# Differential attention and retention in one Trainium2 kernel: the order in which TensorE takes up scores, transposes, sums and outputs

## The chip, the cores and the metric

The kernel runs on one core of one Trainium2 chip. The metric is the device time of one launch in microseconds (us); lower is better. Engine names as in the profile: PE is TensorE (PEld its weight loads), DVE is VectorE, ACT is ScalarE, POOL is GpSimd, SP is SyncE.

## What is computed

Two transformer blocks over 512 tokens of width 1024, in float32. The first mixes a retention branch and a differential attention branch, then runs a mixture of experts; the second has a sliding-window attention and a product-key expert layer. The change touches the two branches of the first block alone:

```python
def retention(q, k, v):                      # 4 heads, dk 128, dv 256, chunks of 128
    s = jnp.einsum('bnihd,bnjhd->bnhij', qc, kc) * dmask      # scores times a decay
    ...
    return (o_in + o_cross).reshape(B, S, H, dv)
ro = head_rms(ro)                            # o * rsqrt(mean(o * o) + EPS), per head

def diff_attention(q, k, v, lam):            # 4 heads, two score maps each
    ...
    p = jax.nn.softmax(s, axis=-1)
    a = p[:, :, 0] - lam * p[:, :, 1]
    return jnp.einsum('bhqk,bkhe->bqhe', a.astype(v.dtype), v)
do = head_rms(do) * diff_norm * (1.0 - lambda_init)
```

## The kernel before

The program is written by hand, engine by engine: each stage is a block with one instruction stream for each engine, and semaphores between them. An engine works through its stream in order, so an instruction that waits holds back all that stand behind it. A stage begins for all engines together when the one before is over.

**`stage_retention`** computes all of retention in its quadratic form, head by head (h = 0 to 3). PE makes four score tiles of the head (`scores(h)`, L585: 128 keys by 512, 384, 256 and 128 queries, two instructions for each in the trace). DVE multiplies them by the decay (`weigh(h)`, L639). PE multiplies by the values into two banks (L597: "output" below). ACT squares both banks (L546) into the buffer `squares`, of which there is one; PE sums the squares over the partitions with a matrix of ones (L604: "total"); ACT takes the root (L550) into `std`, of which there is one; DVE takes the reciprocal (L647) and multiplies both banks by it (L649): "norm" below. The stream of DVE is `weigh(0)`, `weigh(1)`, norm 0, `weigh(2)`, norm 1, `weigh(3)`, norm 2, some sums for lambda, norm 3. The stream of ACT is squares 0, root 0, squares 1, root 1, and so on; squares h wait for total h-1, and root h for norm h-1. `scores(h)` begins with

```python
if h >= 1:
    pe.wait_ge(s.weighted, TT * h)
```

that is, it waits until all of `weigh(h-1)` is done, and the output of head h waits for all of `weigh(h)`.

**`stage_diff`** computes differential attention in 16 units u = (h, t): head h, block t of 128 queries, which sees (t + 1) * 128 keys. For a unit, PE makes the scores of both maps (`scores(u)`, L809), DVE adds the mask and takes the largest (`softmax_max(u)`, L913 to L920, called max), ACT takes exponents with their sums (`exponents(u)`, L874), DVE combines the maps (L928 to L932, called mix), PE transposes the result block by block (`turn(u)`, L819), and ACT copies it out of the one transpose bank (L885). After a head's last unit PE makes the head's output (`output(h)`, L828), ACT squares it (`squares_of`, L860), PE sums (`total`, L837), ACT takes the root (`root_of`, L866), and DVE norms (`normed`, L900 and L902). Two units have score banks and buffers at a time: `scores(u+2)` waits for the exponents of u, and the exponents of u+2 for mix u. DVE's stream is max u+1, mix u, max u+2, mix u+1, and so on; ACT's is exponents u+1, copy u, exponents u+2, copy u+1. In both, the parts of the norm stand at fixed places behind some unit t of the next head. Exponents and roots need different tables of ACT, which shows as ACT_TABLE_LOAD.

Of the kernel before, what the change touches and what calls it, by code (L numbers as in the profile page):

```python
# [26 lines left out]
HEADS = 4  # L27
# [525 lines left out]
def stage_retention(nc, m, qT, kT, vals, roT):  # L553

    with ExitStack() as own:
        sb = lambda name, shape: own.enter_context(nc.sbuf_tensor(name, shape, F32))
        decay = sb("decay", [P, HEADS, T])
        probs = sb("ret_probs", [P, 2, TT, T])
        squares = sb("ret_sq", [P, 2, T])
        std = sb("ret_std", [P, T])  # L560
        lam_in, lam_p = sb("lam_in", [P, 4, P]), sb("lam_p", [P, P])
        lam_s, lam_e = sb("lam_s", [P, 2]), sb("lam_e", [P, 2])
        lam_loaded, lam_ready, lam_exp = (m.sem(f"lam_{x}") for x in ("loaded", "ready", "exp"))
        s = Names()
        s.decay, s.scores, s.weighted, s.out_ready, s.squares, s.total, s.root, s.normed = (
            m.sem(f"ret_{x}") for x in ("decay", "scores", "weighted", "out", "squares", "total", "root", "normed"))
        block = own.enter_context(nc.Block(no_gpsimd_drain=True))

        score = [m.bank[0][:, 0:T], m.bank[1][:, 0:T - P], m.bank[4][:, 0:T - 2 * P], m.bank[1][:, T - P:T]]
        o_banks = [[m.bank[6], m.bank[7]], [m.bank[3], m.bank[5]]]  # L570
        ss_bank = m.bank[2]

        @block.sync
        def _(sp):
            sp.dma_start(decay[:, :, :], m.dram.decay).then_inc(s.decay, 16)
            for i, a in enumerate(m.dram.lams):
                sp.dma_start(lam_in[:, i, :], a.to_broadcast([P, P])).then_inc(lam_loaded, 16)

        @block.tensor
        def _(pe):  # L580
            def scores(h):
                if h >= 1:
                    pe.wait_ge(s.weighted, TT * h)
                for j in range(TT):
                    pe.matmul(score[j], kT[:, h, j * P:(j + 1) * P], qT[:, h, j * P:T],  # L585
                              start=True, stop=True).then_inc(s.scores, 1)

            scores(0)
            for h in range(HEADS):
                if h + 1 < HEADS:  # L590
                    scores(h + 1)
                pe.wait_ge(s.weighted, TT * (h + 1))
                if h >= 2:
                    pe.wait_ge(s.normed, h - 1)
                for c in range(2):
                    for j in range(TT):
                        mm = pe.matmul(o_banks[h % 2][c][:, j * P:T], vals[:, j, h * DV + c * P:h * DV + (c + 1) * P],  # L597
                                       probs[:, h % 2, j, j * P:T], start=(j == 0), stop=(j == TT - 1))
                mm.then_inc(s.out_ready, 1)
                pe.wait_ge(s.squares, 2 * (h + 1))  # L600
                if h >= 1:
                    pe.wait_ge(s.root, h)
                for c in range(2):
                    mm = pe.matmul(ss_bank[:, :], m.ones, squares[:, c, :], start=(c == 0), stop=(c == 1))  # L604
                mm.then_inc(s.total, 1)

        @block.scalar
        def _(act):
            for h in range(HEADS):
                head_norm_act(m, act, o_banks[h % 2], ss_bank, squares, std, h, s)  # L610
            act.wait_ge(lam_ready, 1)
            act.activation(lam_e[:, :], lam_s[:, :], ACT.Exp).then_inc(lam_exp, 1)

        @block.vector
        def _(dve):
            chain = lambda instruction: m.chain(dve, instruction)

            def lambda_sums():
                dve.wait_ge(lam_loaded, 64)
                for i in range(2):  # L620
                    chain(dve.tensor_tensor(lam_p[:, :], lam_in[:, 2 * i, :], lam_in[:, 2 * i + 1, :], ALU.mult))
                    chain(dve.tensor_reduce(lam_s[:, i:i + 1], lam_p[:, :], AX.X, ALU.add))
                dve.sem_inc(lam_ready, 1)
                dve.tensor_scalar(m.dn[:, :], m.dn[:, :], 1.0 - LAMBDA_INIT, None, ALU.mult)

            def lambda_difference():
                dve.wait_ge(lam_exp, 1)
                chain(dve.tensor_tensor(m.neg_lam[:, :], lam_e[:, 1:2], lam_e[:, 0:1], ALU.subtract))
                chain(dve.tensor_scalar(m.neg_lam[:, :], m.neg_lam[:, :], LAMBDA_INIT, None, ALU.subtract))

            dve.wait_ge(s.decay, 16)

            def weigh(h):
                if h >= 2:
                    dve.wait_ge(s.out_ready, h - 1)
                for j in range(TT):

                    dve.wait_ge(s.scores, TT * h + (1 if j == 0 else TT))
                    dve.tensor_tensor(probs[:, h % 2, j, j * P:T], score[j],  # L639
                                      decay[:, h, 0:T - j * P], ALU.mult).then_inc(s.weighted, 1)  # L640

            weigh(0)
            for h in range(HEADS):
                if h + 1 < HEADS:
                    weigh(h + 1)
                dve.wait_ge(s.root, h + 1)
                chain(dve.reciprocal(std[:, :], std[:, :]))  # L647
                for c in range(2):
                    last = dve.tensor_tensor(roT[:, 2 * h + c, :], o_banks[h % 2][c][:, :], std[:, :], ALU.mult)  # L649
                last.then_inc(s.normed, 1)  # L650
                if h == HEADS - 2:
                    lambda_sums()
            lambda_difference()
# [129 lines left out]
def stage_diff(nc, m, qT, kT, vals, doT):  # L783

    units = [(h, t) for h in range(HEADS) for t in range(TT)]
    with ExitStack() as own:
# [4 lines left out]
        squares = sb("diff_sq", [P, 2, T])  # L791
# [10 lines left out]
        @block.tensor  # L802
        def _(pe):
            def scores(u):
                h, t = units[u]
                if u >= 2:
                    pe.wait_ge(s.probs, 2 * (u - 1))
                for c in range(2):
                    mm = pe.matmul(s_bank(u, c)[:, 0:(t + 1) * P], qT[:, 2 * h + c, t * P:(t + 1) * P],  # L809
                                   kT[:, 2 * h + c, 0:(t + 1) * P], start=True, stop=True)  # L810
                mm.then_inc(s.scores, 1)

            def turn(u):
                h, t = units[u]
                pe.wait_ge(s.mixed, u + 1)
                if u >= 1:
                    pe.wait_ge(s.turned_sb, u)
                for j in range(t + 1):
                    mm = pe.transpose(t_bank[:, j * P:(j + 1) * P], p[:, u % 2, 0, j * P:(j + 1) * P], m.ident)  # L819
                mm.then_inc(s.turned, 1)  # L820

            def output(h):
                pe.wait_ge(s.turned_sb, TT * (h + 1))
                if h >= 1:
                    pe.wait_ge(s.normed, h)
                for c in range(2):
                    for j in range(TT):
                        mm = pe.matmul(o_bank[c][:, j * P:T], vals[:, j, h * DV + c * P:h * DV + (c + 1) * P],  # L828
                                       aT[:, j, j * P:T], start=(j == 0), stop=(j == TT - 1))
                mm.then_inc(s.out_ready, 1)  # L830

            def total(h):
                pe.wait_ge(s.squares, 2 * (h + 1))
                if h >= 1:
                    pe.wait_ge(s.root, h)
                for c in range(2):
                    mm = pe.matmul(ss_bank[:, :], m.ones, squares[:, c, :], start=(c == 0), stop=(c == 1))  # L837
                mm.then_inc(s.total, 1)

            scores(0)  # L840
            scores(1)
            for u, (h, t) in enumerate(units):
                if t == 0 and h >= 1:
                    output(h - 1)
                turn(u)
                if u + 2 < len(units):
                    scores(u + 2)
                if t == 1 and h >= 1:
                    total(h - 1)
            output(HEADS - 1)  # L850
            total(HEADS - 1)

        @block.scalar
        def _(act):
# [24 lines left out]
            for u, (h, t) in enumerate(units):  # L879
# [6 lines left out]
                               t_bank[:, 0:(t + 1) * P].rearrange("p (j q) -> p j q", q=P), ACT.Copy).then_inc(s.turned_sb, 1)  # L886
                if t == 0 and h >= 1:
                    squares_of(h - 1)
                if t == 2 and h >= 1:
                    root_of(h - 1)  # L890
            squares_of(HEADS - 1)
            root_of(HEADS - 1)
# [2 lines left out]
        def _(dve):  # L895
# [27 lines left out]
            for u, (h, t) in enumerate(units):  # L923
                if u + 1 < len(units):
# [6 lines left out]
                chain(dve.tensor_scalar(st[:, u % 2, 7:8], st[:, u % 2, 7:8], m.neg_lam[:, :], None, ALU.mult))  # L931
                dve.scalar_tensor_tensor(out=mixed, in0=p[:, u % 2, 1, 0:w], scalar=st[:, u % 2, 7:8], in1=mixed,  # L932
                                         op0=ALU.mult, op1=ALU.add).then_inc(s.mixed, 1)
                if t == 3 and h >= 1:
                    normed(h - 1)
            normed(HEADS - 1)

# [1899 lines left out]
```

## Time and profile before

| | us |
|---|---|
| median of 3 runs | 3022.72 |
| lowest, highest | 3020.35, 3027.94 |
| time of the profiled execution | 3024.56 |
| its span | 3022.8 |
| stage of retention, first instruction of PE to the next stage's first | 164.09 to 217.99 |
| stage of differential attention, the same | 500.13 to 619.28 |
| mean granted clock of PE, as a share of full speed | 0.95 |

The span is the profiled part of that execution; 1.8 us of its time lie around it. Times in rows count from the span's start. The idle time in brackets of a row is what its engine waited before it, with what ended the wait.

### The profile page before, as it was taken

Reading aid. Unit: us, or ns where it says so; the run is one execution under the profiler, and the core shown is the slowest. Engines: PE = TensorE matmul, PEld = TensorE weight load, DVE = VectorE, ACT = ScalarE, POOL = GpSimd, SP = SyncE. Lnnn points to the kernel's source line nnn. Section 1 sums busy time; section 2 is a strip of 40 time slices with the busy share of each in tenths; the row PEclk is TensorE's granted clock in tenths of the full one; section 3 lists DMA queues with packets and bytes.
Section 4 is the critical chain, followed back from the end, with each engine's and each line's share of the span. In section 5 each row is a group of like instructions: output and inputs, shape, how many; then the busy total and the mean of one; then the engine's idle time right before and its main releaser. Section 6 shows DMA issues by size and latency. Waiting matters only on the chain. (4 is left out here: it accounts for less than half of the span.)

```text
span 3022.8 us, 35581 instructions
## 1 busy us (share of the span) xinstructions
PE 2758.4 (91%) x13731; PEld 2399.2 (79%) x13731; DVE 2049.0 (68%) x2757; ACT 1379.6 (46%) x1854; POOL 954.1 (32%) x499
## 2 busy tenths in 40 slices
PE   2979997699699999998778899989999999999999
PEld 1747785377588888885346689989999999999999
DVE  6437571522489888893246368998888777888884
ACT  2223212331377787773134233347887733333332
POOL 1404442023212222230032134743333343444430
PEclk7989998799699999999888999999999999999999
DMA  5225422011399999997331123558999999999993
GB/s 213 84 80 199 163 98 70 0 56 56 143 347 369 387 382 364 357 360 312 116 105 42 59 74 122 171 181 310 346 351 349 340 380 359 376 373 376 369 367 109
DMA packets 171116, 703.95 MB, mean 233 GB/s; under 512 B 24481, under 2 KB 51777, under 8 KB 134593
## 3 DMA queue, kind: packets, MB, share of 16 engines
q1 hardware_dynamic: 86544, 458.44, 41.5%
q0 software_dynamic: 47232, 142.66, 12.8%
q10 hardware_dynamic: 37168, 100.54, 8.9%
q8 instruction: 111, 1.82, 0.2%
q14 instruction: 61, 0.49, 0.0%
HBM read 658.02 MB, written 72.88 MB: 242 GB/s over the span
## 5 line engine op out<-in xcount | busy, mean ns | idle before, releaser
L186 PE MATMUL psum<-h_high,pe_high 128*128 128x384 f32 (+1 forms) x1664 | 570.3, 343 | 11.5 <-DVE h_low L2432 9.2
L187 PE MATMUL psum<-h_low,pe_high 128*128 128x384 f32 (+1 forms) x1664 | 564.2, 339 | 0.0
L188 PE MATMUL psum<-h_high,pe_low 128*128 128x384 f32 (+1 forms) x1664 | 564.0, 339 | 0.0
L2168 ACT ACTIVATE pe_high<-pe_raw 128x1024 fp32r<-128x1024 f32 x272 | 287.1, 1056 | 324.6 <-PE psum L188 324.4
L2295 DVE TENSOR_TENSOR pe_low<-pe_raw,pe_high 128x1024 fp32r<-128x1024 f32 x216 | 264.4, 1224 | 195.8 <-ACT pe_high L2168 189.0
L167 POOL TENSOR_TENSOR slab_low<-half_slab,slab_high 128x1024 fp32r<-128x1024 f32 x84 | 208.5, 2485 | 463.2 <-ACT slab_high L158 463.2
L186 PEld LDWEIGHTS psum<-h_high,pe_high 128*128 128x128 f32 x1664 | 313.4, 188 | 17.3 <-issue 10.0
L1405 DVE TENSOR_TENSOR slab_low_moe<-half_slab_moe,slab_high_moe 128x2048 fp32r<-128x2048 f32 x126 | 285.5, 2287 | 51.8 <-ACT slab_high_moe L1354 51.8
L188 PEld LDWEIGHTS psum<-h_high,pe_low 128*128 128x128 f32 x1664 | 313.1, 188 | 5.2
L187 PEld LDWEIGHTS psum<-h_low,pe_high 128*128 128x128 f32 x1664 | 313.5, 188 | 4.6
L2053 POOL DMA_INDIRECT pe_rows<-in_v_rows,pe_place x128 | 202.0, 1578 | 259.1 <-DVE pe_sums L2402 223.6
L2053 POOL DMA_INDIRECT pe_rows<-in_u_rows,pe_place x128 | 165.3, 1291 | 302.3 <-DVE pe_row_act L2390 286.3
L1354 ACT ACTIVATE slab_high_moe<-half_slab_moe 128x2048 fp32r<-128x2048 f32 x126 | 234.2, 1909 | 25.4 <-issue 25.4
L186 PE MATMUL psum<-h_high,slab_high 128*128 128x512 f32 x448 | 179.3, 400 | 59.5 <-PEq L238 36.8
L2042 POOL TENSOR_TENSOR pe_low<-pe_raw,pe_high 128x1024 fp32r<-128x1024 f32 x56 | 153.8, 2751 | 174.9 <-ACT pe_high L2168 174.7
L158 ACT ACTIVATE slab_high<-half_slab 128x1024 fp32r<-128x1024 f32 x88 | 92.6, 1056 | 252.9 <-PE psum L188 236.0
L186 PE MATMUL psum<-slab_high_moe,moe_x_high 128*128 128x512 f32 x512 | 203.7, 398 | 3.6 <-DVE slab_low_moe L1405 2.2
L188 PE MATMUL psum<-slab_high_moe,moe_x_low 128*128 128x512 f32 x512 | 201.7, 394 | 0.0
L187 PE MATMUL psum<-slab_low_moe,moe_x_high 128*128 128x512 f32 x512 | 201.4, 393 | 0.0
L1260 POOL DMA_INDIRECT y_rows<-moe_y,pairs x32 | 59.1, 1846 | 419.2 <-ACT moe_y L1380 406.3
L187 PE MATMUL psum<-h_low,slab_high 128*128 128x512 f32 x448 | 178.1, 398 | 0.0
L188 PE MATMUL psum<-h_high,slab_low 128*128 128x512 f32 x448 | 177.7, 397 | 0.0
(429 smaller groups left out, 5938.0 us busy)
## 6 DMA issues: line engine op xcount, KB each, us to landing
half_slab_moe<-in_weights SPq DMA_DIRECT2D x128, 1024.0 KB, 7.3
pe_raw<-in_weights SPq DMA_DIRECT2D x144, 512.0 KB
hT<-in_weights SPq DMA_DIRECT2D x64, 1024.0 KB, 7.5
pe_raw<-in_v_rows SPq DMA_DIRECT2D x128, 512.0 KB
half_slab<-in_weights SPq DMA_DIRECT2D x44, 1024.0 KB, 5.2
gates_rows<-pe_table ACTq DMA_DIRECT2D x12, 2048.0 KB
pe_gt<-gates_rows ACTq DMA_DIRECT2D x16, 1536.0 KB
gelu_rows<-pe_gl ACTq DMA_DIRECT2D x30, 768.0 KB
```

What stands on the lines that cost most here:

```text
L158: act.activation(m.high[:, slot, j * w:(j + 1) * w], m.half_slab[:, j // 2, (j % 2) * w:(j % 2 + 1) * w], ACT.Copy).then_inc(m.highs, 1)
L167: pool.tensor_tensor(m.low[:, slot, j * w:(j + 1) * w], m.half_slab[:, j // 2, (j % 2) * w:(j % 2 + 1) * w], m.high[:, slot, j * w:(j + 1) ...
L186: pe.matmul(out, w[0], x[0], start=start, stop=False)
L187: pe.matmul(out, w[0], x[1], start=False, stop=False)
L188: return pe.matmul(out, w[1], x[0], start=False, stop=stop)
L1260: pool.indirect_dma_start(out=d.y_rows, out_offset=bass.IndirectOffsetOnAxis(ap=m.pairs[:, i:i + 1], axis=0), in_=y[:, i % 2, :], in_offse ...
L1354: act.activation(m.high[:, p % 2, h * half:(h + 1) * half], raw(p, h), ACT.Copy).then_inc(m.highs, 2)
L1405: dve.tensor_tensor(m.low[:, p % 2, part], raw(p, h), m.high[:, p % 2, part].bitcast(F32), ALU.subtract).then_inc(m.lows, 2)
L2042: pool.tensor_tensor(low[:, g % RING, :], raw[:, g % RING, :], high[:, g % RING, :].bitcast(F32), ALU.subtract).then_inc(lows_pool, 1)
L2053: pool.indirect_dma_start(out=rows[:, r % ROWS_AHEAD, :], out_offset=None, in_=d.u_rows if r < N else d.v_rows, in_offset=bass.IndirectOff ...
L2168: act.activation(high[:, g % RING, :], raw[:, g % RING, :], ACT.Copy).then_inc(highs, 1)
L2295: dve.tensor_tensor(low[:, g % RING, :], raw[:, g % RING, :], high[:, g % RING, :].bitcast(F32), ALU.subtract).then_inc(lows_dve, 1)
```

## The change

In retention, PE takes up the total of head h-1 behind the output of head h, not the total of head h straight behind the output of head h; the last total follows by itself. In differential attention, PE takes up `scores(u+2)` ahead of the output, the total and `turn(u)`; the total of the head before stands ahead of `turn` at t = 1, not behind it and the scores. The root of the head before moves on ACT from behind t = 2 to behind t = 1, and the norm on DVE from behind t = 3 to behind t = 2. No tile, buffer or matmul is added or taken away.

```diff
--- before.py
+++ after.py
@@ stage_retention, TensorE
+            def total(h):
+                pe.wait_ge(s.squares, 2 * (h + 1))
+                if h >= 1:
+                    pe.wait_ge(s.root, h)
+                for c in range(2):
+                    mm = pe.matmul(ss_bank[:, :], m.ones, squares[:, c, :], start=(c == 0), stop=(c == 1))
+                mm.then_inc(s.total, 1)
+
...
                 mm.then_inc(s.out_ready, 1)
-                pe.wait_ge(s.squares, 2 * (h + 1))
                 if h >= 1:
-                    pe.wait_ge(s.root, h)
-                for c in range(2):
-                    mm = pe.matmul(ss_bank[:, :], m.ones, squares[:, c, :], start=(c == 0), stop=(c == 1))
-                mm.then_inc(s.total, 1)
+                    total(h - 1)
+            total(HEADS - 1)
@@ stage_diff, TensorE
             for u, (h, t) in enumerate(units):
+                if u + 2 < len(units):
+                    scores(u + 2)
                 if t == 0 and h >= 1:
                     output(h - 1)
-                turn(u)
-                if u + 2 < len(units):
-                    scores(u + 2)
                 if t == 1 and h >= 1:
                     total(h - 1)
+                turn(u)
@@ stage_diff, ScalarE
-                if t == 2 and h >= 1:
+                if t == 1 and h >= 1:
                     root_of(h - 1)
@@ stage_diff, VectorE
-                if t == 3 and h >= 1:
+                if t == 2 and h >= 1:
                     normed(h - 1)
```

The first place is PE in retention, from the output of head 0 on (`ret_probs,ret_v`; the total is `ret_sq,const`, the scores are `ret_q,ret_k`). Before:

```order
402 L597 MATMUL psum<-ret_probs,ret_v 128x512
403 L597 MATMUL psum<-ret_probs,ret_v 128x384
404 L597 MATMUL psum<-ret_probs,ret_v 128x256
405 L597 MATMUL psum<-ret_probs,ret_v 128x128
406 L604 MATMUL psum<-ret_sq,const 128x512 x2
407 L585 MATMUL psum<-ret_q,ret_k 128x512
```

The same stretch and what follows it in the changed kernel, up to the first total:

```order
405 L605 MATMUL psum<-ret_probs,ret_v 128x128
406 L585 MATMUL psum<-ret_q,ret_k 128x512
407 L585 MATMUL psum<-ret_q,ret_k 128x384
408 L585 MATMUL psum<-ret_q,ret_k 128x256
409 L585 MATMUL psum<-ret_q,ret_k 128x128
410 L605 MATMUL psum<-ret_probs,ret_v 128x512
...
417 L605 MATMUL psum<-ret_probs,ret_v 128x128
418 L593 MATMUL psum<-ret_sq,const 128x512 x2
419 L585 MATMUL psum<-ret_q,ret_k 128x512
```

The total of head 0 now stands behind the scores of head 2 and the output of head 1, and directly ahead of the scores of head 3.

The second place is PE in differential attention around the start of head 1 (`diff_k,diff_q` are scores, `const,diff_p` transposes, `diff_aT,diff_v` the output, `diff_sq,const` the total). Before:

```order
1606 L819 MATMUL psum<-const,diff_p 128x128 x3
1607 L809 MATMUL psum<-diff_k,diff_q 128x128 x2
1608 L819 MATMUL psum<-const,diff_p 128x128 x4
1609 L809 MATMUL psum<-diff_k,diff_q 128x256 x2
1610 L828 MATMUL psum<-diff_aT,diff_v 128x512
...
1617 L828 MATMUL psum<-diff_aT,diff_v 128x128
1618 L819 MATMUL psum<-const,diff_p 128x128
1619 L809 MATMUL psum<-diff_k,diff_q 128x384 x2
1620 L819 MATMUL psum<-const,diff_p 128x128 x2
1621 L809 MATMUL psum<-diff_k,diff_q 128x512 x2
1622 L837 MATMUL psum<-diff_sq,const 128x512 x2
```

In the changed kernel:

```order
1607 L814 MATMUL psum<-diff_k,diff_q 128x256 x2
1608 L824 MATMUL psum<-const,diff_p 128x128 x4
1609 L814 MATMUL psum<-diff_k,diff_q 128x384 x2
1610 L833 MATMUL psum<-diff_aT,diff_v 128x512
...
1617 L833 MATMUL psum<-diff_aT,diff_v 128x128
1618 L824 MATMUL psum<-const,diff_p 128x128
1619 L814 MATMUL psum<-diff_k,diff_q 128x512 x2
1620 L842 MATMUL psum<-diff_sq,const 128x512 x2
1621 L824 MATMUL psum<-const,diff_p 128x128 x2
```

Each pair of scores stands one transpose group earlier, and the one for t = 2 now ahead of the output.

The third place is ACT in the last head (`diff_p,diff_st` are exponents, `diff_aT` copies, `diff_sq` squares, `diff_std` roots). Before:

```order
125 L874 ACTIVATE diff_p,diff_st<-psum,diff_st 128x512 x2
126 L885 ACTIVATE diff_aT<-psum 128x3x128
127 L866 ACT_TABLE_LOAD
128 L866 ACTIVATE diff_std<-psum,eps 128x512
129 L885 ACTIVATE diff_aT<-psum 128x4x128
130 L860 ACTIVATE diff_sq<-psum 128x512 x2
131 L866 ACTIVATE diff_std<-psum,eps 128x512
```

In the changed kernel:

```order
125 L871 ACT_TABLE_LOAD
126 L871 ACTIVATE diff_std<-psum,eps 128x512
127 L879 ACT_TABLE_LOAD
128 L879 ACTIVATE diff_p,diff_st<-psum,diff_st 128x512 x2
129 L890 ACTIVATE diff_aT<-psum 128x3x128
130 L890 ACTIVATE diff_aT<-psum 128x4x128
131 L865 ACTIVATE diff_sq<-psum 128x512 x2
132 L871 ACT_TABLE_LOAD
133 L871 ACTIVATE diff_std<-psum,eps 128x512
```

The root of head 2 stands ahead of the last exponents, which are the longest, and two table loads are added.

## Rows read from the trace of the kernel before

**Rows 1.** The page, part 4: the chain that ended last, by line

```profile
PE psum L186 11%; PE psum L187 11%; PE psum L188 11%; PE psum L2098 3%; DVE pe_cand L2355 1%; DVE pe_res L2358 1%; DVE pe_cand L2353 1%; DVE pe_pos L2341 0%; DVE pe_pos L2329 0%; DVE pe_cand L2332 0%; PE psum L2077 0%; DVE pe_cand L2323 0%; DVE pe_best L2325 0%; DVE pe_best L2337 0%; PE psum L2104 0%; DVE pe_res L2363 0%
```

**Rows 2.** Windows, both stages: us, busy us of PE, PEld, DVE, ACT, POOL; PEclk

```profile
164.00:218.00 54.00, 37.92 (x113) 21.48 (x113) 26.65 (x35) 8.63 (x15) 0.00 (x0) 0.88 0.12 44
500.10:619.30 119.20, 70.74 (x185) 38.57 (x185) 61.63 (x156) 39.18 (x99) 0.00 (x0) 0.76 0.03 9
```

**Rows 3.** Timeline of retention: start us, us, what, idle before and its end

```profile
172.95 4.55 PE L585 MATMUL psum<-ret_q,ret_k 128*128 128x512 f32 x8 [5.00 <-DVE ret_probs L639]
...
182.99 1.98 PE L604 MATMUL psum<-ret_sq,const 128*128 128x512 f32 x4 [1.18 <-ACT ret_sq L546]
...
184.81 2.32 PE L585 MATMUL psum<-ret_q,ret_k 128*128 128x512 f32 x8
...
185.01 0.69 ACT L550 ACTIVATE ret_std<-psum,eps 128x512 f32<-128x512 f32 x1 [2.08 <-PE psum L604]
...
185.73 3.35 DVE L647 RECIPROCAL ret_std<-ret_std 128x512 f32<-128x512 f32 x1 [7.11 <-ACT ret_std L550]
...
186.96 4.48 PE L597 MATMUL psum<-ret_probs,ret_v 128*128 128x512 f32 x16
...
190.32 1.67 DVE L639 TENSOR_TENSOR ret_probs<-psum,decay 128x512 f32<-128x512 f32 x4
...
192.62 1.98 PE L604 MATMUL psum<-ret_sq,const 128*128 128x512 f32 x4 [1.18 <-ACT ret_sq L546]
...
209.59 0.28 DVE L621 TENSOR_TENSOR lam_p<-lam_in 128x128 f32<-128x128 f32 x1
...
210.98 0.17 DVE L624 TENSOR_SCALAR dn<-dn 128x2 f32<-128x2 f32 x1
```

**Rows 4.** Waits from 500 to 620: engine, line, waited for: us, times, longest

```profile
DVE psum L913 <- PE psum L809: 89.1, 14, 47.5
ACT diff_p L874 <- DVE diff_st L920: 43.4, 14, 5.1
```

**Rows 5.** Timeline of differential attention

```profile
511.74 3.58 PE L809 MATMUL psum<-diff_k,diff_q 128*128 128x512 f32 x4
...
525.92 5.94 PE L828 MATMUL psum<-diff_aT,diff_v 128*128 128x512 f32 x16
...
531.80 1.46 PE L809 MATMUL psum<-diff_k,diff_q 128*128 128x384 f32 x4
...
536.69 3.08 PE L809 MATMUL psum<-diff_k,diff_q 128*128 128x512 f32 x4
...
539.60 1.88 PE L837 MATMUL psum<-diff_sq,const 128*128 128x512 f32 x4
...
544.21 0.50 DVE L913 TENSOR_TENSOR psum<-psum,const 128x128 f32<-128x128 f32 x2 [1.09 <-PE psum L809]
544.27 1.28 ACT L866 ACT_TABLE_LOAD   x1
...
545.57 0.69 ACT L866 ACTIVATE diff_std<-psum,eps 128x512 f32<-128x512 f32 x1
546.18 0.75 DVE L932 SCALAR_TENSOR_TENSOR diff_p<-diff_p,diff_st 128x512 f32<-128x512 f32 x1
...
546.85 3.35 DVE L900 RECIPROCAL diff_std<-diff_std 128x512 f32<-128x512 f32 x1
546.99 1.12 PE L819 MATMUL psum<-const,diff_p 128*128 128x128 f32 x4 [2.81 <-DVE diff_p L932]
...
551.79 6.71 PE L828 MATMUL psum<-diff_aT,diff_v 128*128 128x512 f32 x16 [1.98 <-DVE roT L902]
...
578.71 6.24 PE L828 MATMUL psum<-diff_aT,diff_v 128*128 128x512 f32 x16 [1.98 <-DVE roT L902]
...
603.94 6.25 PE L828 MATMUL psum<-diff_aT,diff_v 128*128 128x512 f32 x16 [5.58 <-DVE roT L902]
...
617.49 1.41 DVE L902 SCALAR_TENSOR_TENSOR roT<-psum,dn,diff_std 128x512 f32<-128x512 f32 x2
```

## The prediction

> **What bounds the kernel now.** I read the chain that ended last first [rows 1]. Its largest entries are L186 to L188, the split matmuls of the weight stages. Neither the retention nor the differential attention stage has a line there, because each is only a few per cent of the span. Stages begin for all engines together, though, so what a stage gains or loses goes into the total one to one: the next stage is a run of matmuls with its weights already split. So each stage is taken as a piece of its own.
>
> In the windows [rows 2] retention takes 54 us with PE busy for 37.9, and differential attention takes 119 us with PE busy for 70.7, DVE for 61.6 and ACT for 39.2. In neither does one engine work throughout. They are loops of waits, and the order of the streams decides.
>
> In retention before, a head takes 192.62 - 182.99 = 9.63 us, and PE sets it: total about 1.8, scores about 2.15, output 4.3 to 4.5, and 1.18 of waiting for the squares [rows 3]. The loop root, norm, `weigh` lies beside it: `weigh(2)` is done at 190.32 + 1.67 = 192.0, while PE needs it only for the output at about 196.6. That is 4.6 us of slack.
>
> In differential attention DVE waits for scores [rows 4]: 89.1 us, of which 47.5 are the wait for the stage to begin, so 41.6 in 13 waits, about 3 us each. PE makes those scores only after `turn(u)`, which waits for mix u. ACT waits 43.4 us for DVE in turn.
>
> **Retention, part by part.** The wait that goes is 1.18 us a head. What is moved costs more. Total h-1 now stands behind output h, and norm h-1 on DVE stands ahead of `weigh(h+1)`, for which scores h+2 and output h+1 wait. The side loop becomes the main one. I walk it with the old durations [rows 3]:
>
> - Output 0 leaves the queue at about 181.6; scores 2 take 2.15, output 1 takes 4.3: 188.05. Only now total 0: 1.75, plus 0.2 until ACT sees it: 190.0 (before: 185.0).
> - Root 0.7, norm 0 from its reciprocal to the next `weigh` 190.32 - 185.73 = 4.6, `weigh(2)` 1.7: 197.0. PE has been idle since 189.8, which is 7.2 us.
> - Scores 3 wait for all of `weigh(2)`. They run at what clock? After an idle of 5.00 us the same four tiles took 4.55 us, against 2.32 for them in a busy stretch [rows 3]: the lower of PE's two levels, 1.2 GHz, and then 2.4. I take 4.0: 201.0. Output 2: 205.3. Total 1, root 1, norm 1, `weigh(3)` in the same way, 1.95 + 0.75 + 4.6 + 1.7 = 9.0: 214.3. PE was idle for 7 us again.
> - Output 3, 4.3 and 1.9 for a slow start: 220.5. Total 2, root 2, norm 2: 1.95 + 0.75 + 4.6, so 227.8. Root 3 needs the one `std` and so norm 2; the lambda sums (209.59 to 211.15, 1.6 [rows 3]) stand ahead of norm 3: 229.4, norm 3 and the lambda difference, 5.0: 234.4.
>
> The change of stage costs some 0.5 (at the end of differential attention the norm ends at 617.49 + 1.41 = 618.90 [rows 5] and PE begins at 619.28), so the next stage's first matmul comes at about 235.0, against 217.99 before. **Retention: +17.0 us.** If PE stayed at full clock over the gaps, it would be 3.7 less, +13.3; with both slow starts at the full difference, about +18.5.
>
> The Trainium skill ("TensorE: Matmul & The Clock Gate", Part 1) says that the throttled clock is the default and that activity releases it. By that rule both restarts behind 7 us are slow, which gives +17; a reading by the busy stretches alone gives +13.3. The trace agrees with the rule, as the 4.55 us behind the 5.00 us gap show.
>
> **Differential attention, part by part.** `scores(u+2)` need the exponents of u, which are there while DVE still mixes u. In their new place they run under that mix, and DVE goes from mix u to max u+2 with no wait. What is left bounds it:
>
> - *Head 0.* DVE's work per head is (61.6 - 4 x 4.76)/4 = 10.6 [rows 2, 5] for four max and four mix, some 11.6 with the gaps between instructions, and max 4 (1.2) comes before output 0. It starts 1.2 us into the stage. Scores 2 and 3 are made at the low clock (3.58 for t = 3 [rows 5]), and DVE still waits about 2.1 for them. Then `turn(3)` 0.9 and scores 6, now ahead of the output, 2.3. Sum 1.2 + 12.8 + 2.1 + 0.9 + 2.3 = 19.3, against 525.92 - 500.13 = 25.8: -6.5.
> - *Heads 1 and 2, output to output.* All of it is now one chain: output 6.1 (the rows have 5.94 to 6.71, each with 0.2 that overlaps what follows), `turn` t = 0 0.1, scores t = 3 2.9, total 1.9, `turn` t = 1 with the step to ACT 0.6, copy 0.4, table load 1.3, root 0.7, norm 3.35 + 1.41 less a little overlap, 4.7, max t = 0 and mix t = 3 together 546.93 - 544.21 = 2.7, `turn` t = 3 0.9, scores t = 2 1.9 (1.46 at full clock, double at half) [rows 5]. That is 24.2. Before, the output starts lie 25.87 and 26.92 apart, 52.8 for both: -4.4. The second table load and the exponents behind root (1.3 + 1.45) lie under the norm's 4.7 and cost nothing. They would cost if the norm were under 2.8.
> - *Head 3 to output 3.* The same chain without max and scores but with the last copy: 6.1 + 0.1 + 2.9 + 1.9 + 0.6 + 0.4 + 1.3 + 0.7 + 4.7 + 1.6 + 0.9 + 0.9 = 22.1, against 603.94 - 578.71 = 25.23: -3.1. The final output, squares, total, root and norm stay, 603.94 to 618.90; the added table load lies in ACT's 2.1 us wait for the last total.
>
> Sum: **-14.0**. It rests on PE's clock, which is 0.76 here [rows 2]. At full clock the output takes 4.4, scores 1.9 and 1.46, total 1.75, `turn` 0.5: some 3.3 less a head and 2 less in head 0, so about -26. With PE at the low level in every burst but the second half of an output (6.5, 3.6, 2.6, 0.8, 1.1 and 2.75 for those terms) a head takes 27.3 and the stage gains only about 4. PE's gaps get shorter for most units and stay at some 3.5 us around the root and norm, so I expect the clock of before or a little better: -16, with -11 to -22 as bounds.
>
> For the table loads the Trainium skill ("ScalarE: Activation LUTs", What ACT_TABLE_LOAD costs) has 1.28 us and a drain of 1.38 more for each switch. The one before the root would then cost three heads 4.1 us more, and the gain would be -12. The trace does not show the drain here: the load starts at 544.27, and the root starts at 545.57 [rows 5], 1.30 later; the row decides.
>
> **Sum.** +17.0 - 16 = +1. The profiled execution took 3024.56 (span 3022.8, 1.8 around it), which gives 3025.6; it was 1.8 above the median of its runs, 3022.72, so the same sum against the median gives 3023.7. A change of 0.3% is 9 us, about what a measurement of this kernel can tell from none.
>
> **Rivals.**
>
> - *The two cancel* (0.72): +13.3 to +18.5 and -11 to -22; 3014 to 3030, likeliest 3024.
> - *PE warms up in the denser differential stage* (0.12). For it: the loop loses most of its 3 us gaps. Against: the gap at the root and norm stays, and output 1 began cold behind such a gap. Gain -22 to -26 with +13.3 to +17: 3010 to 3018, around the bound.
> - *PE stays cold in the differential stage* (0.12), the case that ends slower. Place: every output and score pair behind the norm of a head. Price: 27.3 us a head, -4 in all, +17 in retention: 3035.7. It decides once the head's chain is above some 26 us. By the clock rule of the page named above this is what gaps do. The time here comes from the rows alone, which show both levels in this stage.
> - *Retention's norm loop is hidden after all* (0.04): if `weigh` didn't stand behind the norm, only the removed waits (4 x 1.18) and the differential gain would show, 3002. Against it stands the order of DVE's stream, norm 0 ahead of `weigh(2)`.
>
> The range 3013 to 3033 holds the first case and about half of each of the two beside it. Faster by over 0.3% (under 3013.6): the last case and half of the second, 0.11. Slower by over 0.3% (above 3031.8): most of the third, 0.12. Within: 0.77.
>
> **What would show it.** In retention: PE idle for about 7 us before scores 3 and before output 3, ended by DVE L639; the stage 17 us longer; DVE still with few waits between root and norm. In differential attention: DVE's waits for scores fall from 41.6 us to some 15 to 20 and sit at the outputs; outputs 24 us apart; output 0 at 19 us into the stage; the stage at 103 us. All stages behind keep their lengths. I am wrong if `weigh(2)` ends before PE wants it, or if the clock in either stage differs much from 0.76.

## The result and the profile after

| | before | changed |
|---|---|---|
| median of 20 runs each, us | 3025.80 | 3021.43 |
| lowest, highest | 3020.35, 3033.99 | 3016.12, 3026.20 |
| time and span of the profiled execution | 3024.56, 3022.8 | 3023.46, 3021.7 |
| stage of retention, first matmul to the next stage's first | 53.90 | 71.38 |
| stage of differential attention, the same | 119.15 | 94.92 |

The ratio of the changed kernel to the one before is 0.9985, with a 95% interval of 0.9979 to 0.9992: 4.5 us faster, between 2.4 and 6.4. I had forecast 3024.0, a microsecond slower. The time lies in the range, and within 0.3% of no change; the direction was wrong. The forecast counted from 3022.72, the median of the three runs known then; that of 20 runs is 3025.80, so a change of +1 would have been some 3027.

The page of the changed kernel looks like that of before, and its chain by line is the one of [rows 1] with shifted line numbers. The two stages differ widely, one up by 17.5 us and the other down by 24.2. Their windows, as in [rows 2]:

```profile
164.80:236.20 71.40, 42.22 (x113) 23.26 (x113) 26.57 (x35) 8.29 (x15) 0.00 (x0) 0.79 0.09 33
518.20:613.10 94.90, 60.62 (x184) 35.01 (x185) 61.34 (x156) 40.95 (x101) 0.00 (x0) 0.81 0.03 11
```

PE works longer in retention for the same matmuls (42.2 us against 37.9), and shorter in differential attention (60.6 against 70.7). The granted clock goes with it: 0.79 in place of 0.88 in the first, 0.81 in place of 0.76 in the second.

Retention after, timeline (the columns of [rows 3]):

```profile
189.03 1.88 PE L593 MATMUL psum<-ret_sq,const 128*128 128x512 f32 x4
190.95 0.69 ACT L550 ACTIVATE ret_std<-psum,eps 128x512 f32<-128x512 f32 x1 [7.11 <-PE psum L593]
...
191.67 3.35 DVE L652 RECIPROCAL ret_std<-ret_std 128x512 f32<-128x512 f32 x1 [12.37 <-ACT ret_std L550]
...
196.26 1.68 DVE L644 TENSOR_TENSOR ret_probs<-psum,decay 128x512 f32<-128x512 f32 x4
197.99 4.59 PE L585 MATMUL psum<-ret_q,ret_k 128*128 128x512 f32 x8 [7.08 <-DVE ret_probs L644]
202.42 4.48 PE L605 MATMUL psum<-ret_probs,ret_v 128*128 128x512 f32 x16
206.73 1.88 PE L593 MATMUL psum<-ret_sq,const 128*128 128x512 f32 x4
...
215.69 6.43 PE L605 MATMUL psum<-ret_probs,ret_v 128*128 128x512 f32 x16 [7.08 <-DVE ret_probs L644]
...
236.20 0.77 PE L186 MATMUL psum<-h_high,slab_high 128*128 128x512 f32 x1 [8.61 <-PEq L555]
```

Total, root, norm, `weigh(2)`, scores 3 stand in one line, and PE is idle twice for 7.08 us until DVE L644. A total follows a total after 17.70 us (189.03 to 206.73), against 9.63 before. Behind either gap PE starts at its low clock: 4.59 us for scores 3, where 2.32 is full clock [rows 3], and 6.43 for output 3, where 4.48 is.

Differential attention after, the scores of t = 3 in head 0, then from one output to the next and on to the last:

```profile
523.88 1.88 PE L814 MATMUL psum<-diff_k,diff_q 128*128 128x512 f32 x4
...
534.87 4.48 PE L833 MATMUL psum<-diff_aT,diff_v 128*128 128x512 f32 x16
...
553.05 1.12 PE L824 MATMUL psum<-const,diff_p 128*128 128x128 f32 x4 [2.63 <-DVE diff_p L937]
553.96 2.77 PE L814 MATMUL psum<-diff_k,diff_q 128*128 128x384 f32 x4
...
556.51 4.92 PE L833 MATMUL psum<-diff_aT,diff_v 128*128 128x512 f32 x16
...
561.38 1.88 PE L814 MATMUL psum<-diff_k,diff_q 128*128 128x512 f32 x4
...
563.10 1.88 PE L842 MATMUL psum<-diff_sq,const 128*128 128x512 f32 x4
...
566.93 0.69 ACT L871 ACTIVATE diff_std<-psum,eps 128x512 f32<-128x512 f32 x1
...
567.65 3.35 DVE L905 RECIPROCAL diff_std<-diff_std 128x512 f32<-128x512 f32 x1 [1.03 <-ACT diff_std L871]
...
575.13 1.11 PE L824 MATMUL psum<-const,diff_p 128*128 128x128 f32 x4 [3.18 <-DVE diff_p L937]
...
578.24 4.48 PE L833 MATMUL psum<-diff_aT,diff_v 128*128 128x512 f32 x16
...
595.41 1.12 PE L824 MATMUL psum<-const,diff_p 128*128 128x128 f32 x4 [6.91 <-DVE diff_p L937]
...
597.22 6.81 PE L833 MATMUL psum<-diff_aT,diff_v 128*128 128x512 f32 x16 [0.69 <-ACT diff_aT L890]
```

The outputs lie 21.6 and 21.7 us apart where [rows 5] has 25.9 and 26.9. Those of heads 1 and 2 now take 4.92 and 4.48 us, where they took 6.71 and 6.24. The waits, as in [rows 4]:

```profile
DVE psum L918 <- PE psum L814: 61.2, 8, 47.4
...
ACT diff_p L879 <- DVE diff_st L925: 10.6, 6, 2.9
...
PE psum L814 <- ACT diff_p L879: 6.9, 3, 3.2
```

DVE's waits for scores inside the stage fell from 41.6 us to 61.2 - 47.4 = 13.8. PE now waits three times for exponents: twice 3.2 us behind the table loads around a root, and once 0.45 in head 0.

### The profile page after: what moved, and what is told of

Same layout as the page of the kernel before. It is cut to its first block and busy times, and to the rows that moved or that the text cites. A ratio compares the mean times of both kernels' runs of the same rounds, so it can differ in the third digit from the quotient of the medians.

```text
span 3021.7 us, 35583 instructions
## 1 busy us (share of the span) xinstructions
PE 2754.8 (91%) x13731; PEld 2399.5 (79%) x13731; DVE 2046.3 (68%) x2757; ACT 1381.0 (46%) x1856; POOL 958.2 (32%) x499
## 3 DMA queue, kind: packets, MB, share of 16 engines
q1 hardware_dynamic: 86544, 458.44, 41.6%
## 5 line engine op out<-in xcount | busy, mean ns | idle before, releaser
L186 PEld LDWEIGHTS psum<-h_high,pe_high 128*128 128x128 f32 x1664 | 313.4, 188 | 17.3 <-issue 10.0
```

The lines of the kernel that those rows point to most:

```text
L186: pe.matmul(out, w[0], x[0], start=start, stop=False)
```

## The experiments

The theory before the runs: retention's loss is the order alone, as predicted. In differential attention the order gives what I had summed, and the rest of the gain is PE's clock. The rival: the order gives all 24 us. The times below are ratios to the kernel before, in us of 3026; the stage times are those of the one trace of each kernel. In traces without an edit in the differential stage it took 119.05 to 121.20 us, so a trace tells 2 us there.

**E1, retention alone; E2, differential attention alone.** Each is one half of the diff above, with the other stage as before.

> Retention in the changed order, differential attention as before. Theory (the norm of a head stands ahead of the next weigh on VectorE, so the delayed total delays scores, output and everything behind): the retention stage takes 71.4 us as in the changed kernel, +17.5, and the time is 15 to 19 us above the kernel before. Rival (the two stages influence each other, or the loss was partly one of that execution): under 12 us.

> Differential attention in the changed order, retention as before. Theory: that stage takes about 94.9 us from its first matmul to the next stage's, 24.2 less than before, and the time is 21 to 26 us under the kernel before. Rival (my term of -16 was right and the rest is one lucky execution's clock): 14 to 18 us under, the stage at 101 to 105 us.

E1: ratio 1.0076 (1.0062 to 1.0089), +23 us (19 to 27); its stage took 71.18 us, 17.3 more. E2: 0.9925 (0.9911 to 0.9938), -23 us (19 to 27); its stage took 97.23 us, 21.9 less. Either half acts by itself. The loss of E1's stage is that of the theory, but its whole time is above the 15 to 19 that I gave and above the stage's loss by more than its interval allows, and nothing in the one trace (span 3040.4, 17.6 more) shows where. The traced execution was the shortest of E1's five; the others have spans of 3044.1 to 3049.1. Added up, the whole times of the halves give 0, with some 6 us of uncertainty either way: that holds the 4.5 us, but doesn't tell the direction. The 20 runs of each kernel do.

**E3, the scores alone moved ahead.** Total, root and norm stay where they were:

```diff
@@ stage_diff, TensorE
             for u, (h, t) in enumerate(units):
+                if u + 2 < len(units):
+                    scores(u + 2)
                 if t == 0 and h >= 1:
                     output(h - 1)
                 turn(u)
-                if u + 2 < len(units):
-                    scores(u + 2)
                 if t == 1 and h >= 1:
                     total(h - 1)
```

> Retention as before; in differential attention only the scores of u+2 move ahead of output and transposes, while total, root and norm stay at their old places (total behind the transposes of t = 1, root behind t = 2, norm behind t = 3). Theory (the scores carry the whole gain, and the norm one unit ahead puts root, two table loads and 4.7 us of norm into the head's chain): the stage takes 87 to 91 us, and the time is 28 to 32 us under the kernel before, some 6 us better than with all of it moved. Rival (the earlier norm is part of the gain): the stage takes over 97 us and the time is less than 22 us under.

0.9901 (0.9886 to 0.9917), -30 us (25 to 34). The stage took 88.41 us: 30.7 less than before, and 6.5 to 8.8 less than with all of the change. The theory holds by the stage: two lines carry more than the whole gain, and the rest of the change gives some of it back. The whole times of E3 and E2 don't tell the two apart, since their intervals overlap; the 6.5 to 8.8 us rest on one trace of each kernel.

**E7, scores, root and norm moved, the total not.** E2 with `total(h - 1)` behind `turn(u)`:

```diff
@@ stage_diff, TensorE, against E2
-                if t == 1 and h >= 1:
-                    total(h - 1)
                 turn(u)
+                if t == 1 and h >= 1:
+                    total(h - 1)
```

> The changed order of differential attention except that the total of the head before stays behind the transposes of t = 1; root and norm are one unit early as in the change; retention as before. Theory (both the early total and the early root and norm cost, about half each, of the 6 to 9 us between 88.4 with the scores alone and 94.9 to 97.2 with all): the stage takes 90 to 93 us. Rival (the early norm alone costs it all): 94 us or more.

0.9905 (0.9890 to 0.9920), -29 us. The stage took 93.18 us, just outside the span that I gave. Root and norm one unit early cost 4.8 us against E3, and the early total 1.7 to 4.0 more. With 2 us between traces of one stage, it isn't shown which is the larger share, and the whole times of E7 and E3 are the same within their intervals.

**E4, retention with `weigh` ahead of the norm.**

```diff
@@ stage_retention, VectorE, against E1
             weigh(0)
+            weigh(1)
             for h in range(HEADS):
-                if h + 1 < HEADS:
-                    weigh(h + 1)
+                if h + 2 < HEADS:
+                    weigh(h + 2)
```

> Retention in the changed order of TensorE, but VectorE takes up weigh of head h+2 ahead of the norm of head h; differential attention as before. Theory (what costs is weigh and scores standing behind the norm): the scores of head 3 no longer wait, only the outputs do, for the bank that the norm frees; the stage takes 61 to 64 us, +8 to +10 on the kernel before, 8 to 9 less than with the changed order alone. Rival (the late total itself costs, whatever VectorE's order is): no better than the changed order alone, +15 to +18.

1.0047 (1.0033 to 1.0061), +14 us. The stage took 68.18 us, not 61 to 64. The timeline of PE shows why:

```profile
197.87 7.62 PE L605 MATMUL psum<-ret_probs,ret_v 128*128 128x512 f32 x16 [3.42 <-DVE roT L655]
...
212.78 6.99 PE L605 MATMUL psum<-ret_probs,ret_v 128*128 128x512 f32 x16 [5.58 <-DVE roT L655]
```

In place of two gaps of 7.08 us, ahead of scores 3 and output 3, there are 3.42 and 5.58 ahead of outputs 2 and 3. Behind them both outputs ran at the low clock ("cold" below), 7.6 and 7.0 us, where 4.5 is full clock: 5.6 us together, more than the cold starts of E1 cost. So only 3.0 us are left of what VectorE's order wins over E1 (71.18 - 68.18), and the rival, that the late total itself costs, isn't out.

**E12, the same with fillers.** Fillers are matmuls whose result nobody reads; they keep PE at work where it would wait. Here they go into the bank of the total, behind the root that reads it; the next total overwrites them.

```diff
@@ stage_retention, TensorE, against E4
+                if h >= 2:
+                    pe.wait_ge(s.root, h - 1)
+                    for _ in range(3 if h == 2 else 5):
+                        pe.matmul(ss_bank[:, :], m.ones, decay[:, 0, :], start=True, stop=True)
                 pe.wait_ge(s.weighted, TT * (h + 1))
```

> Retention with the changed order of TensorE, weigh ahead of the norm on VectorE, and fillers in the two idle stretches ahead of outputs 2 and 3. Differential attention as before. Theory (the walk for weigh first was right in order, 61 to 64 us, and missed only that outputs 2 and 3 started cold, 7.4 and 6.8 us in place of 4.3): the stage takes 62 to 63.5 us against 68.2. Rival (something else in that loop costs): 66 us or more.

1.0034 (1.0021 to 1.0048), +10 us. The stage took 62.08 us, 6.1 less than E4, and the two outputs 4.55:

```profile
196.56 4.55 PE L609 MATMUL psum<-ret_probs,ret_v 128*128 128x512 f32 x16 [0.85 <-DVE roT L659]
...
208.41 4.55 PE L609 MATMUL psum<-ret_probs,ret_v 128*128 128x512 f32 x16 [0.24 <-DVE roT L659]
```

Order and clock are apart now: with both mended the late total still costs 8.2 us (62.08 - 53.90). Up to the start of output 3 it is 3.5 us, where outputs 2 and 3 wait for the bank that a norm frees. The other 4.7 lie behind: from output 3 to the next stage it takes 18.62 us (208.41 to 227.03), against 13.92 before (204.07 to 217.99), since total 2, root 2 and norm 2 now come only behind output 3, and root 3 and norm 3 behind them.

**E8, retention in the changed order with fillers.**

```diff
@@ stage_retention, TensorE, against E1
+                if h >= 2:
+                    pe.wait_ge(s.root, h - 1)
+                    for _ in range(6):
+                        pe.matmul(ss_bank[:, :], m.ones, decay[:, 0, :], start=True, stop=True)
                 if h + 1 < HEADS:
                     scores(h + 1)
```

> Retention in the changed order with six filler matmuls of 512 columns ahead of the scores of head 3 and of the output of head 3, where TensorE sat idle for 7.1 us; they write the bank of the total behind its root, and it is overwritten before it is read again. Differential attention as before. Theory (of the 17.5 us, 3.7 to 4.5 are the low clock behind the two idle stretches, the rest the order): the stage takes 66.5 to 68 us in place of 71.3. Rival (the slow starts have another cause, or the norm's loop hides them): 70 us or more.

1.0041 (1.0026 to 1.0056), +12 us. The stage took 67.72 us, 3.7 less than the changed kernel's and 3.5 less than E1's, against the 3.7 of the prediction:

```profile
198.77 2.42 PE L585 MATMUL psum<-ret_q,ret_k 128*128 128x512 f32 x8 [0.88 <-DVE ret_probs L648]
...
214.31 4.58 PE L609 MATMUL psum<-ret_probs,ret_v 128*128 128x512 f32 x16 [0.88 <-DVE ret_probs L648]
```

So the retention term of 17.5 splits into 13.8 us of order and 3.7 of clock. Of the order, 5.6 are `weigh` and scores behind the norm (67.72 - 62.08, both with fillers), and 8.2 are the late total itself, which E12 still has.

**E5 and E6, fillers ahead of every wait for the mix.** In E5 on the kernel before, in E6 on E3:

```diff
@@ stage_diff, TensorE, turn(u)
-                pe.wait_ge(s.mixed, u + 1)
                 if u >= 1:
                     pe.wait_ge(s.turned_sb, u)
+                for _ in range(2):
+                    pe.matmul(t_bank[:, :], m.ones, vals[:, 0, 0:T], start=True, stop=True)
+                pe.wait_ge(s.mixed, u + 1)
```

> The kernel before, with two filler matmuls of 512 columns ahead of each wait of TensorE for the mix, so that it works on where it sat idle; they write the transpose bank, whose content is overwritten, so the result doesn't depend on them. Theory (some 8 to 10 of the 24 us that the differential stage gained come from TensorE's clock, the rest from the order): the granted clock of the stage rises from 0.76 to over 0.9 and the stage falls from 119.2 us to 107 to 113. Rival (the clock was no part of it, the order alone gave 24): the stage stays within 2 us of 119, or gets longer by the fillers.

> The scores alone moved ahead (retention, total, root and norm as before) and the same two fillers ahead of the wait for the mix. Theory (clock and order add up, what is left at the low clock is still worth a few us): the stage takes 82 to 87 us, against 88.4 without fillers. Rival (TensorE has so little idle time left that the fillers now stand in the way of transposes and scores): 89 us or more.

E5: 0.9983 (0.9974 to 0.9992), the stage 114.47 us at a clock of 0.90. That is neither expectation: 4.7 less. E6: 0.9926 (0.9912 to 0.9939), the stage 98.08 us at a clock of 0.95, 9.7 longer than E3, as the rival said. With fillers in every unit, those behind an output or a total hold up transposes that were ready, mostly by the 1.7 us that two fillers take. The experiment mixed clock and obstruction, so I made it again.

**E9 and E10, fillers fitted to the gaps.** E9 is the kernel before with fillers only where PE waits, in the transpose bank. E10 is E2 with five around root and norm, in the total's bank.

```diff
@@ E9: stage_diff, TensorE, turn(u), as E5 but
+                for _ in range((2, 2, 2, 2)[t] if h == 0 else (0, 2, 0, 2)[t]):
@@ E9: output(h), ahead of the wait for the norm
+                    for _ in range((0, 2, 2, 5)[h]):
+                        pe.matmul(t_bank[:, :], m.ones, vals[:, 0, 0:T], start=True, stop=True)
@@ E10: at t = 3 of heads 1 to 3
+                if t == 3 and h >= 1:
+                    pe.wait_ge(s.root, h)
+                    for _ in range(3):
+                        pe.matmul(ss_bank[:, :], m.ones, vals[:, 0, 0:T], start=True, stop=True)
                 if u + 2 < len(units):
                     scores(u + 2)
+                if t == 3 and h >= 1:
+                    for _ in range(2):
+                        pe.matmul(ss_bank[:, :], m.ones, vals[:, 0, 0:T], start=True, stop=True)
```

> The kernel before with filler matmuls in the differential stage at the places where TensorE waits for the mix or the norm, sized so that they end before what they fill is over (none behind an output or a total, more ahead of the outputs of heads 1 to 3); they write the transpose bank and are overwritten. Theory (at full clock the old order takes some 12 us less, and about 9 of the changed order's 24 are clock): the stage takes 104 to 109 us at a granted clock over 0.9. Rival (the clock is worth the 5 us that the first fillers showed, no more): 112 us or more.

> The changed order of differential attention alone, with fillers in the two idle stretches of TensorE around root and norm (three ahead of the scores at t = 3 of heads 1 to 3, behind the root, and two ahead of the transposes there), written to the total's bank between root and next total. Theory (what is left of the low clock is in the output of the next head and the scores ahead of it): the stage takes 89 to 92 us against 94.9 and 97.2 in the two traces without. Rival (the low clock left is all in head 0, which has no fillers here, or the fillers stand in the way): 94 us or more.

E9: 0.9957 (0.9942 to 0.9973), -13 us, its stage as expected. E10: 0.9904 (0.9888 to 0.9920), -29 us, its stage 0.4 us under what I gave. The window of the stage, first of E9:

```profile
500.50:605.60 105.10, 81.14 (x242) 41.25 (x243) 61.69 (x156) 39.35 (x99) 0.00 (x0) 0.94 0.03 11
```

and of E10:

```profile
502.60:591.20 88.60, 66.55 (x214) 36.23 (x215) 61.13 (x156) 41.17 (x101) 0.00 (x0) 0.94 0.04 12
```

At one and the same clock of 0.94 the old order takes 105.1 us and the new one 88.6: **16.5 us are the order**, if no filler stands in the way. In E9 some do: norm 2 is over at 588.50 + 1.41 = 589.91, but output 3, which needs it, starts at 592.03, when the five fillers ahead of it are done. These 2.1 us lie in the chain, so the order is worth 14.4 to 16.5. In E10 PE still waits for the mix behind the fillers of each head (1.8 us), so there they held up nothing in the chain.

The low clock cost at least 14.0 us in the old order (119.15 - 105.13), or 16.1 without those 2.1, and costs 6.3 to 8.6 in the new one (94.92 and 97.23, against 88.64). What is left of the stage's 24.2 or 21.9 beside the order is clock: 5.4 to 7.7 us with the order at 16.5, up to 9.8 with it at 14.4. In E9 the outputs behind a norm show it:

```profile
544.36 4.58 PE L832 MATMUL psum<-diff_aT,diff_v 128*128 128x512 f32 x16 [0.80 <-DVE roT L906]
...
567.44 4.58 PE L832 MATMUL psum<-diff_aT,diff_v 128*128 128x512 f32 x16 [0.60 <-DVE roT L906]
...
592.03 4.48 PE L832 MATMUL psum<-diff_aT,diff_v 128*128 128x512 f32 x16
```

They took 6.71, 6.24 and 6.25 in [rows 5].

**E11, the best of it: the scores alone ahead, with fitted fillers.** E3's outputs behind a norm:

```profile
536.90 5.24 PE L828 MATMUL psum<-diff_aT,diff_v 128*128 128x512 f32 x16
...
555.44 6.21 PE L828 MATMUL psum<-diff_aT,diff_v 128*128 128x512 f32 x16
...
574.94 6.69 PE L828 MATMUL psum<-diff_aT,diff_v 128*128 128x512 f32 x16 [5.38 <-DVE roT L902]
```

```diff
@@ stage_diff, TensorE, against E3
+                if t == 0 and h >= 2:
+                    pe.wait_ge(s.root, h - 1)
+                    for _ in range(2):
+                        pe.matmul(ss_bank[:, :], m.ones, vals[:, 0, 0:T], start=True, stop=True)
                 if u + 2 < len(units):
                     scores(u + 2)
                 if t == 0 and h >= 1:
+                    if h >= 2:
+                        for _ in range(1):
+                            pe.matmul(ss_bank[:, :], m.ones, vals[:, 0, 0:T], start=True, stop=True)
                     output(h - 1)
...
+            pe.wait_ge(s.root, HEADS - 1)
+            for _ in range(5):
+                pe.matmul(ss_bank[:, :], m.ones, vals[:, 0, 0:T], start=True, stop=True)
             output(HEADS - 1)
```

> Retention as before, the scores alone moved ahead, and fillers only where TensorE waits for a norm or for exponents: two ahead of the scores of t = 2 and one ahead of the output (heads 1 and 2), five ahead of the last head's output, all into the total's bank behind the root. Theory (here too the outputs behind a norm ran at the low clock, 5.2 to 6.7 us in place of 4.5): the stage takes 84 to 86 us against 88.4, and the time is 33 to 36 us under the kernel before, the lowest of all. Rival (what the first fillers showed, that they stand in the way, holds here too): 88 us or more.

0.9894 (0.9879 to 0.9909), -32 us (28 to 37), median 2994.0: the lowest of all, a little short of the 33 to 36 that I gave, and below the changed kernel by 27, some 17 of them because retention stays as it was. The stage took 85.46 us (502.88 to 588.34), and the same outputs:

```profile
537.97 4.48 PE L828 MATMUL psum<-diff_aT,diff_v 128*128 128x512 f32 x16
...
555.74 4.55 PE L828 MATMUL psum<-diff_aT,diff_v 128*128 128x512 f32 x16 [0.39 <-DVE roT L912]
...
574.76 4.48 PE L828 MATMUL psum<-diff_aT,diff_v 128*128 128x512 f32 x16
```

Its lead on E3, 2.95 us of stage, is too small for the whole time to tell the two apart.

## Why the prediction missed the direction

**Retention: right, +17.0 against +17.5.** Each step is in the trace: the idle stretches (7.2 foretold, 7.08), output 3 (6.2 foretold, 6.43), norm 3 behind the lambda sums. E12 and E8 show the shares: 5.6 us for `weigh` and scores behind the norm, 8.2 for the late total itself, 3.7 for the clock. The rival that hid the norm's loop is out. The clock rule of the Trainium skill ("TensorE: Matmul & The Clock Gate", Part 1) chose rightly between +13.3 and +17; the two starts behind the 7.08 us gaps were slow.

**Differential attention: the term of -16 was mis-sized; it measured -24.2 and, in E2's trace, -21.9.** The step that failed is "the clock of before or a little better". The order was worth 14.4 to 16.5 us in E9 and E10, where the sum at the clock of before had 14.0; the clock came on top with 5.4 to 9.8, where I had put 2.

By the terms, in the changed kernel's trace: in the chain from output to output I had put 6.1 for the output, 2.9 for the scores of t = 3 and 1.9 for the total. They took 4.8, 1.7 and 1.7 (starts at 556.51, 561.27, 561.38, 563.10, 564.81). These 2.7 us a head account for all of the 24.2 less 21.7. The other terms were right within 0.3: table load to norm 2.0, norm 4.7, max and mix 2.7, `turn` 0.9, scores of t = 2 2.2. Head 0 took 16.7 us to its output where I had put 19.3: its scores of t = 3 ran at full clock (1.88, not 3.58), and its last scores took 1.3, not 2.3. The stretch to output 3 took 19.0, not 22.1.

I had let the cold start of [rows 5] at 551.79 stand for the new order too. There, though, the output began behind a gap of 1.98 us, among the old gaps of 3 us in every unit: from 547.0 to 551.7 PE was busy for 2.8 us at a granted clock of 0.50, and the output, to 558.4, had 0.67. In the new order transposes, scores of t = 2 and output run without a gap (553.05 to 561.3). The granted clock is still 0.50 up to the output of head 1, and 0.91 in it; in head 2 it is 0.54 and then 1.00. So the longest block of the head takes the benefit. The head that still has a long gap, the last, is the exception: behind 6.91 us of idle and the last transposes its output took 6.81.

The second rival had this mechanism, with -22 to -26 in the stage; I gave it 0.12 and should have given it more. It was not, as I thought, enough to bring a 0.3% gain: its 3010 to 3018 counted from 3022.72, and from the median of 20 runs, 3025.80, it would have been 3013 to 3021.

**The table loads.** By the Trainium skill ("ScalarE: Activation LUTs", What ACT_TABLE_LOAD costs) each switch costs a drain besides the load. The changed kernel's trace has the load start at 565.63 and the root at 566.93, 1.30 us later, so the drain doesn't show in this chain.

**What I left out.** I asked what the early root and norm do to the sum, found them hidden under each other, and stopped. I didn't ask what the stage would do without them. E3's stage shows 6.5 to 8.8 us there, more than the whole net gain.

**The sum.** +17.5 - 24.2 = -6.7 from one pair of traces, and +17.3 - 21.9 = -4.6 from E1's and E2's; measured -4.5 (2.4 to 6.4). The stages behind took 2403.5 us before and 2408.6 after. In the 14 traces they range from 2400.8 to 2408.6 with no relation to the edit, so the 5.1 us between these two is no effect of the change. What stays open is why E1's whole time lies 1.5 us or more above what its stage accounts for.

## What to carry to other kernels

Moving a consumer behind unrelated work on its engine is free only while nobody downstream feeds that engine: walk the loop once around, here total, root, norm, `weigh`, scores, total, before calling a wait removed. When a loop of short waits is tightened on TensorE, price the matmuls behind it at full clock as well as at the measured one, and when a gap is opened, price the restart. And take a change that moves three things apart: here the scores of differential attention alone were better than all of it.

## What the runs showed of the hardware

- A gap can cost nearly its own length again: behind an idle of 3.42 us in E4 an output took 7.6 us in place of 4.5. Fillers of 2.7 us of matmuls in that gap (E12) brought 4.55.
- Fillers pay only in real gaps: two matmuls in every unit took 4.7 us off the stage (E5), and fillers fitted to its waits 14.0 (E9); in a loop with few gaps left, two in every unit cost 9.7 (E6).
